# GLA input, gate and output projections as three products of rounded operands instead of full-precision products, with each weight panel's remainder written over the panel in the load ring

## The chip, the cores and the metric

One core of a Trainium2 chip runs the whole program. TensorE multiplies (PE in the rows, PEld for its weight loads), VectorE (DVE) and ScalarE (ACT) do the elementwise work, GpSimd (POOL) does little, and SyncE (SP) issues the loads from HBM. The metric is the device time of one execution in microseconds (us).

## What is computed

Two transformer blocks follow each other on 256 tokens of width 1024, all in float32. The change touches the first layer of the second block, a gated linear attention (GLA). Cut to that:

```
def gla_mixer(h, w_in, w_g2, b_g2, norm_g, w_out):
    proj = h @ w_in
    q, k, v, og, gl = jnp.split(proj, [H * dk, 2 * H * dk, 2 * H * dk + H * dv, 2 * H * dk + 2 * H * dv], axis=-1)
    log_a = jax.nn.log_sigmoid((gl @ w_g2 + b_g2).astype(jnp.float32)) / GLA_GATE_TAU
    ...
    b = jnp.cumsum(log_a.reshape(shp), axis=2)
    q_t = q * jnp.exp(b)
    k_t = k * jnp.exp(-b)
    k_dec = k * jnp.exp(b_last - b)
    scores = jnp.einsum('bnchd,bnmhd->bnhcm', q_t, k_t)
    ...
    o = rmsnorm_2(o, norm_g) * jax.nn.silu(og.reshape(bsz, s_len, H, dv).astype(jnp.float32))
    return (o.reshape(bsz, s_len, H * dv) @ w_out).astype(h.dtype)
```

Here H = 4 heads, dk = 128, dv = 256, and the recurrence runs over chunks of 64 tokens. The layer stands between the feed-forward part of the first block and a retrieval layer over 16384 small experts (`peer`), which takes most of the kernel's time and is not touched.

## The kernel before

Every engine has its own program, written out by hand in order, and they meet through named semaphores. Nothing is reordered by a scheduler: an engine that waits holds back everything behind it.

Weights come as panels of 128 x 2048 float32 (1 MB) into a ring of four slots. SP loads panel n into slot n mod 4 as soon as panel n-4 is freed, and takes the panels in one fixed order. In the GLA layer this order is a panel of `gla_qk` and a panel of `kv_mod` four times, then `gla_v` and `kv_mod` four times, then four of `gla_og`, four of `gla_out` and those of `peer_wq`. A GLA panel is freed when PE has finished its two output tiles (semaphore `proj`). A `kv_mod` panel belongs to another product, which DVE computes one column block at a time (`mod_between` on DVE, L1683 and L1686, eight instructions); it is freed by `mod_acc` when DVE is done, and PE then adds it up over partitions with two small matmuls (L502, `mod_between` on PE) between two GLA panels.

On PE a GLA tile is 8 matmuls of 128 x 128 weights by 256 tokens in float32. The q and k panels go through `proj_cols` (L532), the v panels through `proj_rows` (L542), the og panels through `og_tiles` (L996) spread between the steps of the attention, and the output panels through `proj_cols` again (L532). The tiles alternate between two banks of PSUM, 4 and 5, so that a tile can start only when ACT has copied out (L1139) the tile before the last; for the output panels DVE does this in `residual` (L1728).

Before the panels, the gate projection (`wgl`, 16 columns, L972, then L978) runs. ACT turns its result into the gate's logarithm (L1499 to L1503), DVE sums it up along the tokens (L2305 to L2313) and clears a buffer (L2314), and ACT takes the exponentials (L1508 to L1511, `exps`) between the copies of the q tiles and those of the k tiles. After the attention DVE takes the root of the norm (`roots`, L1775 and L1778) and multiplies the eight blocks of the output by gate and root (`gate_block` L1798, L1809, semaphore `o_done`), which the output projection reads.

Elsewhere the kernel already computes products as three: an operand is rounded to the `f32r` format by a copy on ACT, the remainder is the operand less that copy, taken on DVE or POOL, and PE adds up high x high, high x remainder and remainder x high.

## Time and profile before

| | us |
|---|---|
| median of 3 runs | 2584.69 (2582.22 to 2589.7) |
| the profiled execution's own time | 2585.32 |
| its span in the trace | 2583.5 |
| PE busy | 2500.4 |
| DVE busy | 1780.5 |
| ACT busy | 1239.6 |
| GLA panels in the trace | from 584.9 to 723.9 |

Times in the trace are counted from the span's start. A matmul in float32 shows as two records, so that a tile of 8 is a row with x16; a tile in three products would be x24, one record each. Busy time of PE counts overlapping records once.

### The profile page before, as it was taken

The page shows a single profiled execution, that of the slowest core. Times are in us where ns is not written, and L with a number is a line of the kernel's source. Part 1 is how long each engine was busy: PE and PEld are TensorE (multiplying, and loading weights), DVE is VectorE, ACT ScalarE, POOL GpSimd, SP SyncE. Part 2 cuts the span into 40 slices and gives each one's busy share as a digit, 9 for nine tenths or more (in the row PEclk, how much of TensorE's full clock was granted, in tenths as well). Part 3 has the DMA queues.
Part 4 walks back from the last instruction along what each step waited for, and adds up shares of the span by engine and source line. Part 5 has one row for each costly group of instructions (what it writes and reads, how often), then busy time and mean ns, then how long its engine had stood idle before and what let it go on. Part 6 is the DMA issues. An engine that isn't in the chain of part 4 may idle for free.

```text
span 2583.5 us, 43038 instructions
## 1 busy us (share of the span) xinstructions
PE 2500.4 (97%) x15948; PEld 2246.5 (87%) x15948; DVE 1780.5 (69%) x3565; ACT 1239.6 (48%) x2429; POOL 79.4 (3%) x42
## 2 busy tenths in 40 slices
PE   7999999999999999999999998989999999999997
PEld 4587889988889999999888887789999999888886
DVE  5672668866359977786788875739987787555554
ACT  2322124432234567775444444433557776455444
POOL 0000000000050000000000000022000000000000
PEclk9999999999999999999999999999999999999998
DMA  6562567656343554444777764233554444555553
GB/s 265 197 243 82 204 221 278 237 219 228 115 144 137 181 179 138 141 146 151 259 279 275 274 233 162 82 115 115 180 181 150 144 142 140 193 195 192 190 191 110
DMA packets 65352, 471.70 MB, mean 183 GB/s; under 512 B 7296, under 2 KB 7552, under 8 KB 8240
## 3 DMA queue, kind: packets, MB, share of 16 engines
q1 hardware_dynamic: 64656, 467.85, 50.5%
q8 instruction: 106, 1.74, 0.3%
q10 hardware_dynamic: 272, 1.05, 0.1%
q0 software_dynamic: 272, 0.69, 0.1%
q14 instruction: 46, 0.38, 0.0%
HBM read 468.51 MB, written 1.05 MB: 182 GB/s over the span
## 4 chain that ended last, share of the span: by engine, by line
PE 86%; DVE 6%; DMA 1%; ACT 1%; issue 1%; DVEq 0%; SPq 0%; ACTq 0%
PE bank L745 27%; PE bank L670 27%; PE bank L902 5%; PE bank L682 4%; PE bank L532 4%; PE bank L811 4%; PE bank L697 3%; PE bank L933 2%; PE bank L996 1%; PE bank L542 1%; PE bank L1039 1%; DVE macc L1686 1%; PE bank L516 1%; PE bank L809 1%; PE bank L548 1%
## 5 line engine op out<-in xcount | busy, mean ns | idle before, releaser
L670 PE MATMUL bank<-h_split,t_split 128*128 128x256 f32 x6144 | 772.2, 285 | 6.2 <-DVE t_split L1918 4.9
L670 PEld LDWEIGHTS bank<-h_split,t_split 128*128 128x128 f32 x6144 | 745.5, 191 | 8.5 <-DVE t_split L1918 6.1
L1918 DVE TENSOR_TENSOR t_split<-ring,t_split 128x1024 fp32r<-128x1024 f32 x512 | 624.7, 1221 | 160.7 <-ACT t_split L1212 159.3
L745 PE MATMUL bank<-t_split,w_split 128*128 128x512 f32 x3072 | 703.9, 390 | 0.0
L745 PEld LDWEIGHTS bank<-t_split,w_split 128*128 128x128 f32 x3072 | 574.8, 188 | 118.8
L1217 ACT ACTIVATE t_split<-ring 128x1024 fp32r<-128x1024 f32 x256 | 271.6, 1061 | 357.8 <-PE bank L745 288.7
L1212 ACT ACTIVATE t_split<-ring 128x1024 fp32r<-128x1024 f32 x256 | 271.1, 1059 | 295.8 <-PE bank L670 275.2
L1950 DVE TENSOR_TENSOR w_split<-arena,w_split 128x256 fp32r<-128x256 f32 x256 | 108.8, 425 | 223.5 <-ACT w_split L1219 223.5
L1139 ACT ACTIVATE arena<-bank 128x256 f32<-128x256 f32 (+2 forms) x160 | 64.3, 405 | 326.6 <-PE bank L697 67.0
L1686 DVE SCALAR_TENSOR_TENSOR macc<-ring,cact,macc 128x256 f32<-128x256 f32 x336 | 162.9, 485 | 12.0
L902 PE MATMUL bank<-h_split,wd_split 128*128 128x256 f32 x1056 | 130.1, 284 | 4.0 <-ACT h_split L1439 4.0
L902 PEld LDWEIGHTS bank<-h_split,wd_split 128*128 128x128 f32 x1056 | 127.2, 192 | 5.5 <-issue 4.3
L532 PE MATMUL bank<-arena,ring 128*128 128x256 f32 x512 | 113.7, 381 | 4.2 <-DVE H L2206 2.2
L532 PEld LDWEIGHTS bank<-arena,ring 128*128 128x128 f32 x512 | 96.3, 190 | 18.3 <-DVE H L2206 3.0
L697 PE MATMUL bank<-h_split,q_split 128*128 128x256 f32 x768 | 100.6, 292 | 8.0 <-ACT h_split L1199 7.9
L697 PEld LDWEIGHTS bank<-h_split,q_split 128*128 128x128 f32 x768 | 96.3, 196 | 10.6 <-issue 8.7
L1219 ACT ACTIVATE w_split<-arena 128x256 fp32r (+1 forms) x256 | 102.7, 401 | 0.0
L811 PE MATMUL bank<-H,ring 128*128 128x256 f32 x448 | 100.6, 381 | 1.1 <-DMA ring<-in_w_in 0.8
L811 PEld LDWEIGHTS bank<-H,ring 128*128 128x128 f32 x448 | 83.8, 190 | 12.8 <-DMA ring<-in_w_in 1.0
L532 PE MATMUL bank<-H,ring 128*128 128x512 f32 (+1 forms) x256 | 86.9, 500 | 3.0 <-ACT H L1328 2.3
L2462 POOL TENSOR_TENSOR q_split<-ring,q_split 128x1024 fp32r<-128x1024 f32 x32 | 75.8, 2393 | 317.4 <-ACT q_split L1189 317.4
L1430 ACT ACTIVATE wd_split<-ring 128x1024 fp32r<-128x1024 f32 x44 | 44.1, 1053 | 84.7 <-DMA ring<-in_w_up 55.7
(302 smaller groups left out, 2768.9 us busy)
## 6 DMA issues: line engine op xcount, KB each, us to landing
ring<-in_peer_u SPq DMA_DIRECT2D x128, 1024.0 KB, 4.9
ring<-in_peer_v SPq DMA_DIRECT2D x128, 1024.0 KB, 4.9
ring<-in_w_mod SPq DMA_DIRECT2D x24, 1024.0 KB, 5.1
ring<-in_mod_w SPq DMA_DIRECT2D x24, 1024.0 KB, 4.9
arena<-in_mod_w SPq DMA_DIRECT2D x24, 1024.0 KB, 6.5
ring<-in_w_in SPq DMA_DIRECT2D x22, 1024.0 KB, 4.9
ring<-in_w_up SPq DMA_DIRECT2D x22, 1024.0 KB, 5.1
ring<-in_peer_wq SPq DMA_DIRECT2D x16, 1024.0 KB, 4.9
```

Source lines behind the costliest of these rows:

```text
L532: last = mm(bank[:, 0:width], w[:, k, j * P:(j + 1) * P], rhs(k), start=(k == 0), stop=(k == ks - 1))
L670: last = mm(bank[:, 0:T], u[:, a_, k, :], h_split[:, b_, k, :], start=(k == 0 and a_ + b_ == 0), stop=(k == KT - 1 and a_ == 1))
L682: last = mm(BK[6 + b][:, j * P:(j + 1) * P], P2[b][:, j, :], P1[b][:, j, :], start=True, stop=True)
L697: last = mm(banks[j][:, 0:T], w[:, a_, k, j * P:(j + 1) * P], h_split[:, b_, k, :], start=(first and k == 0), stop=(last_one and k == KT - 1))
L745: last = mm(BK[2 * tt + hf][:, :], w_split[:, j, a_, tt * P:(tt + 1) * P], t_split[:, 1 - j, b_, hf * 512:(hf + 1) * 512], start=(first an ...
L811: last = mm(bank[:, 0:T], w[:, k, half], Hx[:, k, :], start=(k == 0), stop=(k == KT - 1))
L902: last = mm(banks[j][:, 0:T], w[:, a_, k, j * P:(j + 1) * P], h_split[:, b_, k, :], start=(first and k == 0), stop=(last_one and k == KT - 1))
L1212: A(t_split[:, 1 - j, 0, :].rearrange("p (k c) -> p k c", k=KT), ring[:, r, :].rearrange("p (k j c) -> p j k c", k=KT, j=2)[:, j], ACT.Cop ...
L1217: A(t_split[:, 1 - j, 0, :].rearrange("p (k c) -> p k c", k=KT), ring[:, r, :].rearrange("p (j k c) -> p j k c", k=KT, j=2)[:, j], ACT.Cop ...
L1686: ins = STT(acc, w[:, k, :], cact[:, c_col + k:c_col + k + 1], acc, MUL, ADD)
L1918: TT(t_split[:, 1 - j, 1, :].rearrange("p (k c) -> p k c", k=KT), ring[:, r, :].rearrange(view, k=KT, j=2)[:, j], t_split[:, 1 - j, 0, :]. ...
L1950: TT(w_split[:, b % 2, 1, :], arena[:, bass.ds(at * T, T)], w_split[:, b % 2, 0, :].bitcast(f32), SUB).then_inc(sems["w_ready"], 1)
```

## The change

The 16 GLA panels (`GLA[0]` to `GLA[15]`: four q and k, four v, four og, four output) and the gate's weights are multiplied as three products. For panel p, ACT writes the rounded copy in two halves into `g_hi`, which has two buffers (`hi_g`); DVE then writes the remainder over the panel in its ring slot, seen as `ring_lo` (`lo_g`); and PE runs each tile as 24 matmuls (`gla_tile`): it waits for the copy before the first 16 and for the remainder before the last 8 of a panel's first tile. The layer's input gets a remainder too (`h_lo`), and so does the attention's output, block by block (`o_hi` on ACT, `o_lo` on DVE). The program is written in another order only where these calls stand between others. The order of the loads and what frees a slot stay. Lines of before and after differ by some dozens; the main ones after are L1018 (matmuls of a panel), L1173 (copies out of a bank), L1190 (`hi_g`), L1754 and L1757 (`mod_between` on DVE), L1869 (`lo_g`), L1875 (`o_rest`).

```diff
+            pe.wait_ge(sems["wgl_hi"], 1)
             bank = ring_bank()
-            for k in range(KT):
-                fresh(k)
-                last = mm(bank[0:16, 0:T], wgl[:, k, :], hT[:, k, :], start=(k == 0), stop=(k == KT - 1))
+            for a_, b_ in ((0, 0), (1, 0), (0, 1)):
+                if a_ == 1:
+                    pe.wait_ge(sems["wgl_lo"], 1)
+                for k in range(KT):
+                    if a_ == 0:
+                        fresh(k, 1, "h_lo" if b_ else "h")
+                    last = mm(bank[0:16, 0:T], wgl_split[:, a_, k, :], h_split[:, b_, k, :],
+                              start=(a_ == b_ == k == 0), stop=(b_ == 1 and k == KT - 1))
             last.then_inc(sems["turn"], 1)
             pe.wait_ge(sems["wg2_in"], e.more("wg2_in", 16))
             pe.wait_ge(*e.tile_out())
@@ -977,25 +993,42 @@
                 bank = ring_bank()
                 mm(bank[:, 0:T], M3["wg2"][0:16, h * P:(h + 1) * P], M3["glT"][0:16, :], start=True, stop=True).then_inc(sems["turn"], 1)
             mod_start(0)
-            for _ in range(4):
-                proj_cols(1, lambda k: hT[:, k, :], T)
+            def gla_tile(p, j):
+                if j == 0:
+                    pe.wait_ge(sems["gla_hi"], 2 * p + 2)
+                    e.skip(f"loaded{panel[0] % RING}", 16)
+                    panel[0] += 1
+                wh = g_hi[:, p % 2, :].rearrange("p (k c) -> p k c", k=KT)
+                wl = ring_lo[:, GLA[p] % RING, :].rearrange("p (k c) -> p k c", k=KT)
+                part = slice(j * P, (j + 1) * P)
+                bank = ring_bank()
+                for w, b_ in ((wh, 0), (wh, 1), (wl, 0)):
+                    if w is wl and j == 0:
+                        pe.wait_ge(sems["gla_lo"], p + 1)
+                    for k in range(KT):
+                        if p == 12 and j == 0 and w is wh:
+                            fresh(k, 1, "o_lo" if b_ else "o_hi")
+                        if p < 4 or 8 <= p < 12:
+                            lhs, rhs = w[:, k, part], h_split[:, b_, k, :]
+                        elif p < 8:
+                            lhs, rhs = h_split[:, b_, k, part], w[:, k, :]
+                        else:
+                            lhs, rhs = w[:, k, part], (o_lo if b_ else o_hi)[:, k, :]
+                        last = mm(bank[:, 0:T], lhs, rhs, start=(w is wh and b_ == k == 0), stop=(w is wl and k == KT - 1))
+                last.then_inc(sems["proj"], 1)
+            for p in range(8):
+                for j in range(2):
+                    gla_tile(p, j)
                 mod_between(1)
-            for _ in range(4):
-                proj_rows(1, lambda k, tt: hT[:, k, tt * P:(tt + 1) * P], 2)
-                mod_between(1)
-            og_panel = [None, 0]
+            og_now = [0]
             def og_tiles(n):
                 for _ in range(n):
-                    j = og_panel[1] % 2
-                    if j == 0:
-                        og_panel[0] = next_panel().rearrange("p (k c) -> p k c", k=KT)
-                    bank = ring_bank()
-                    for k in range(KT):
-                        last = mm(bank[:, 0:T], og_panel[0][:, k, j * P:(j + 1) * P], hT[:, k, :], start=(k == 0), stop=(k == KT - 1))
-                    last.then_inc(sems["proj"], 1)
-                    og_panel[1] += 1
+                    gla_tile(8 + og_now[0] // 2, og_now[0] % 2)
+                    og_now[0] += 1
             vN3 = M3["vN"].rearrange("p (t n) -> p t n", t=2)
...
+            def hi_g(p):
+                m = GLA[p]
+                act.wait_ge(sems[f"loaded{m % RING}"], 16 * (m // RING + 1))
+                for j in range(2):
+                    half = slice(j * D, (j + 1) * D)
+                    A(g_hi[:, p % 2, half], slot(m)[:, half], ACT.Copy).then_inc(sems["gla_hi"], 1)
             def std_root():
...
@@ -1188,11 +1232,23 @@
                         half = slice(j * D, (j + 1) * D)
                         A(q_split[:, h % 2, 0, half], slot(m)[:, half], ACT.Copy).then_inc(sems["q_hi"], 1)
+                def split_14():
+                    hi_g(14)
+                    hi_q(0)
+                def split_15():
+                    hi_g(15)
+                    hi_q(1)
                 if l == 0:
                     act.wait_ge(sems["o_done"], 1 + 8)
-                hi_q(0)
-                hi_q(1)
-                squares(xT, hP, "proj")
+                    squares(xT, hP, "proj", {1: split_14, 3: split_15})
+                else:
+                    hi_q(0)
+                    hi_q(1)
+                    squares(xT, hP, "proj")
                 std_root()
                 for k in range(KT):
...
@@ -1484,9 +1541,12 @@
             act.wait_ge(sems["var"], e.more("var"))
             A(nrm[:, 1, :], nrm[:, 1, :], ACT.Sqrt, scale=1.0 / D).then_inc(sems["std"], 1)
             A(nrm[:, 0, :], nrm[:, 0, :], ACT.Sqrt).then_inc(sems["xstd"], 1)
+            act.wait_ge(sems["wgl_in"], 16)
+            A(wgl_split[:, 0, :, :], wgl, ACT.Copy).then_inc(sems["wgl_hi"], 1)
             for k in range(KT):
                 act.wait_ge(sems["hs"], e.more("hs"))
-                A(hT[:, k, :], hT[:, k, :], ACT.Identity, bias=modc[:, k:k + 1]).then_inc(sems["h"], 1)
+                A(h_split[:, 0, k, :], hT2[:, k, :], ACT.Identity, bias=modc[:, k:k + 1]).then_inc(sems["h"], 1)
+            hi_g(1)
             evac_gl = 4 + e.tile % 2
             e.tile += 1
             act.wait_ge(sems["turn"], e.more("turn"))
@@ -1503,6 +1563,8 @@
             A(M3["zB"], M3["zB"], ACT.Ln, bias=ones[:, 0:1]).then_inc(sems["zln"], 1)
             for h in range(4):
                 evac("proj", kt(M3["q"], 4)[:, h, :], ACT.Copy, scale=float(P) ** -0.5)
+                if h % 2:
+                    hi_g(2 + h // 2)
             act.wait_ge(sems["expo"], e.more("expo"))
             tau = 1.0 / 16.0
             A(M3["qi0"], M3["cum0"], ACT.Exp, scale=tau)
@@ -1512,16 +1574,21 @@
               scale=tau).then_inc(sems["exps"], 1)
             for h in range(4):
                 evac("proj", kt(M3["k"], 4)[:, h, :], ACT.Copy)
+                if h % 2:
+                    hi_g(4 + h // 2)
             vN3 = M3["vN"].rearrange("p (t n) -> p t n", t=2)
             for c in range(4):
                 for tt in range(2):
                     evac("proj", vN3[:, tt, c * 2 * P:(c + 1) * 2 * P], ACT.Copy)
+                hi_g(6 + c)
             og_now = [0]
             def og_tiles(n):
                 for _ in range(n):
                     evac("proj", kt(M3["og"], 8)[:, og_now[0], :], ACT.Silu)
+                    if og_now[0] % 2 and og_now[0] < 7:
+                        hi_g(10 + og_now[0] // 2)
                     og_now[0] += 1
             lin_turned(M3, 0, 1)
@@ -1535,6 +1602,10 @@
             og_tiles(1)
             lin_root(M3["zA"])
             og_tiles(4)
+            for b in range(KT):
+                act.wait_ge(sems["o_done"], 1 + b + 1)
+                A(o_hi[:, b, :], kt(M3["oT"], 8)[:, b, :], ACT.Copy).then_inc(sems["o_hi"], 1)
+            hi_g(13)
             peer(0, 32, 24)
...
@@ -1787,6 +1860,19 @@
                 ins.then_inc(sems["dve_step"], 1)
                 dve.wait_ge(sems["dve_step"], e.stepped())
                 TT(M1["oT"], M1["oT"], M1["og"], MUL).then_inc(sems["o_done"], 1)
+            def lo_g(p):
+                for j in range(2):
+                    half = slice(j * D, (j + 1) * D)
+                    dve.wait_ge(sems["gla_hi"], 2 * p + j + 1)
+                    ins = TT(ring_lo[:, GLA[p] % RING, half], slot(GLA[p])[:, half], g_hi[:, p % 2, half].bitcast(f32), SUB)
+                ins.then_inc(sems["gla_lo"], 1)
+            def o_rest(b):
+                dve.wait_ge(sems["o_hi"], b + 1)
+                TT(o_lo[:, b, :], kt(M3["oT"], 8)[:, b, :], o_hi[:, b, :].bitcast(f32), SUB).then_inc(sems["o_lo"], 1)
             def gated(root_buf, dv):
@@ -1807,6 +1893,12 @@
                     if b >= 4:
                         dve.wait_ge(sems["dve_step"], gate_block(b))
                     TT(oT[:, b, :], oT[:, b, :], root_buf[:, b // 2 * T:(b // 2 + 1) * T], MUL).then_inc(sems["o_done"], 1)
+                    if b == 1:
+                        lo_g(12)
+                    if b:
+                        o_rest(b - 1)
+                o_rest(7)
+                lo_g(13)
             iota16 = iota[:, 0:16].unsqueeze(1).broadcast_to([P, P, 16])
...
@@ -2291,7 +2383,14 @@
             dve.reciprocal(macc[:, 2, :], nrm[:, 1, :]).then_inc(sems["dve_step"], 1)
             dve.wait_ge(sems["dve_step"], e.stepped())
             for k in range(KT):
-                STT(hT[:, k, :], xT[:, k, :], gain[:, 0, k:k + 1], macc[:, 2, :], MUL, MUL).then_inc(sems["hs"], 1)
+                STT(hT2[:, k, :], xT[:, k, :], gain[:, 0, k:k + 1], macc[:, 2, :], MUL, MUL).then_inc(sems["hs"], 1)
+            dve.wait_ge(sems["wgl_hi"], 1)
+            TT(wgl_split[:, 1, :, :], wgl, wgl_split[:, 0, :, :].bitcast(f32), SUB).then_inc(sems["wgl_lo"], 1)
+            for k in range(KT):
+                dve.wait_ge(sems["h"], GL_H * KT + k + 1)
+                STT(h_split[:, 1, k, :], hT2[:, k, :], modc[:, k:k + 1], h_split[:, 0, k, :].bitcast(f32), ADD, SUB
+                    ).then_inc(sems["h_lo"], 1)
+            lo_g(0)
             dve.wait_ge(sems["xstd"], 1)
             dve.reciprocal(nrm[:, 0, :], nrm[:, 0, :]).then_inc(sems["dve_step"], 1)
             dve.wait_ge(sems["dve_step"], e.stepped())
@@ -2314,6 +2413,7 @@
             dve.memset(M3["sc"], 0.0).then_inc(sems["dve_step"], 1)
             dve.wait_ge(sems["dve_step"], e.stepped())
             for n in range(4):
+                lo_g(n + 1)
                 used(1)
                 mod_between(1, 16)
             e.tiles("proj", 8)
@@ -2323,8 +2423,10 @@
             TT(M3["ki0"], M3["ki0"], M3["k"], MUL)
             TT(M3["kd0"], M3["kd0"], M3["k"], MUL).then_inc(sems["lin_in"], 1)
             for n in range(4):
+                lo_g(n + 5)
                 used(1)
                 mod_between(1, 16)
+            lo_g(9)
             mod_out(0, 16, V("kv_mod_b"), dst=kvm)
             used(4)
             e.tiles("proj", 8)
@@ -2334,8 +2436,15 @@
                 for _ in range(tiles):
                     e.tiles("proj", 1)
                     og_out.append(e.tile_out())
-            lin(M3, 1, 2, M3["zA"], 2 * P, lambda d, h: None, gated)
-            residual("proj", 16)
+            def behind_gated(h):
+                if h == 0:
+                    lo_g(10)
+                if h == 3:
+                    lo_g(11)
+            lin(M3, 1, 2, M3["zA"], 2 * P, lambda d, h: None, gated, behind_gated)
+            residual("proj", 16, also={1: lambda: lo_g(14), 3: lambda: lo_g(15)})
             used(4)
             peer(0)
```

DVE between the end of the gate's sums and the first `kv_mod` panels, before (L2305 to L2313 are the sums, L2314 clears the buffer, L1683 and L1686 are one `kv_mod` panel):

```order
L2305 SCALAR_TENSOR_TENSOR arena<-arena 128x1024
L2309 SCALAR_TENSOR_TENSOR arena<-con,arena 128x256 x4
L2313 TENSOR_TENSOR arena<-arena 128x1024
L2314 MEMSET arena 128x1024
L1683 TENSOR_SCALAR macc<-ring,cact 128x256
L1686 SCALAR_TENSOR_TENSOR macc<-ring,cact,macc 128x256 x7
```

and after:

```order
L2404 SCALAR_TENSOR_TENSOR arena<-arena 128x1024
L2408 SCALAR_TENSOR_TENSOR arena<-con,arena 128x256 x4
L2412 TENSOR_TENSOR arena<-arena 128x1024
L2413 MEMSET arena 128x1024
L1869 TENSOR_TENSOR ring_lo<-ring,g_hi 128x1024 x2
L1754 TENSOR_SCALAR macc<-ring,cact 128x256
L1757 SCALAR_TENSOR_TENSOR macc<-ring,cact,macc 128x256 x7
```

The remainder of panel 1 stands behind the sums and the clearing, and in front of the first `kv_mod` panel; those of panels 2 to 8 stand likewise in front of the later ones.

ACT from the gate's logarithm to the copies of the k tiles, before (the copies out of a bank are L1139; L1508 to L1511 are the exponentials):

```order
L1503 ACTIVATE arena<-arena,con 128x1024
L1139 ACTIVATE arena<-bank 128x256 x4
L1508 ACT_TABLE_LOAD
L1508 ACTIVATE arena<-arena 128x1024
L1509 ACTIVATE arena<-arena 128x1024
L1510 ACTIVATE arena<-arena 128x1024
L1511 ACTIVATE arena<-arena 128x16
L1139 ACTIVATE arena<-bank 128x256 x13
```

and after:

```order
L1563 ACTIVATE arena<-arena,con 128x1024
L1173 ACTIVATE arena<-bank 128x256 x2
L1190 ACTIVATE g_hi<-ring 128x1024 x2
L1173 ACTIVATE arena<-bank 128x256 x2
L1190 ACTIVATE g_hi<-ring 128x1024 x2
L1570 ACT_TABLE_LOAD
L1570 ACTIVATE arena<-arena 128x1024
L1571 ACTIVATE arena<-arena 128x1024
L1572 ACTIVATE arena<-arena 128x1024
L1573 ACTIVATE arena<-arena 128x16
L1173 ACTIVATE arena<-bank 128x256 x2
```

The rounded copies of panels 2 and 3 now stand among the copies of the q tiles, and that of panel 3 in front of the exponentials and of the copies of the k tiles.

DVE behind the root's reciprocal, at the output's blocks, before (L1809 is a block times the root, L1798 a block times its gate):

```order
L1778 RECIPROCAL arena<-arena 128x1024
L1809 TENSOR_TENSOR arena<-arena 128x256 x4
L1798 SCALAR_TENSOR_TENSOR arena<-arena,vec 128x256
L1809 TENSOR_TENSOR arena<-arena 128x256
L1798 SCALAR_TENSOR_TENSOR arena<-arena,vec 128x256
```

and after:

```order
L1851 RECIPROCAL arena<-arena 128x1024
L1895 TENSOR_TENSOR arena<-arena 128x256 x2
L1869 TENSOR_TENSOR ring_lo<-ring,g_hi 128x1024 x2
L1875 TENSOR_TENSOR o_lo<-arena,o_hi 128x256
L1895 TENSOR_TENSOR arena<-arena 128x256
L1875 TENSOR_TENSOR o_lo<-arena,o_hi 128x256
L1895 TENSOR_TENSOR arena<-arena 128x256
L1875 TENSOR_TENSOR o_lo<-arena,o_hi 128x256
L1884 SCALAR_TENSOR_TENSOR arena<-arena,vec 128x256
L1895 TENSOR_TENSOR arena<-arena 128x256
```

Panel 12's remainder and one remainder for each block now stand between the products that finish the blocks.

## Rows read from the trace of the kernel before

**Rows 1.** The page, part 1: busy us, share of the span, instructions.

```profile
PE 2500.4 (97%) x15948; PEld 2246.5 (87%) x15948; DVE 1780.5 (69%) x3565; ACT 1239.6 (48%) x2429; POOL 79.4 (3%) x42
```

**Rows 2.** Windows: us, busy by engine, granted clock, DMA share, GB/s.

```profile
584.00:724.00 140.00, 135.77 (x709) 118.11 (x709) 64.86 (x122) 37.02 (x63) 9.33 (x4) 1.00 0.47 173
```

**Rows 3.** Timeline, two v panels 14.70 us apart: start, length, engine, line, count.

```profile
617.14 7.15 PE L542 MATMUL bank<-ring,H 128*128 128x256 f32 x32
...
631.84 7.15 PE L542 MATMUL bank<-ring,H 128*128 128x256 f32 x32
```

**Rows 4.** Timeline of PE: two tiles in three products, then the keys.

```profile
765.93 5.85 PE L697 MATMUL bank<-h_split,q_split 128*128 128x256 f32 x48
771.62 1.05 PE L651 MATMUL bank<-small,arena 128*128 128x128 f32 x8
```

**Rows 5.** Timeline: a panel of `w_up` split, copy on ACT, remainder on DVE.

```profile
399.94 2.00 ACT L1430 ACTIVATE wd_split<-ring 128x1024 fp32r<-128x1024 f32 x2
...
401.02 2.36 DVE L2220 TENSOR_TENSOR wd_split<-ring,wd_split 128x1024 fp32r<-128x1024 f32 x2
```

**Rows 6.** Timeline: the layer's input, the gate projection, the first GLA panels.

```profile
575.67 3.26 DVE L2294 SCALAR_TENSOR_TENSOR H<-xT,gain,macc 128x256 f32<-128x256 f32 x8
...
576.85 4.92 PE L972 MATMUL bank<-H,arena 128*16 128x256 f32 x16 [4.43 <-ACT H L1489]
...
581.80 0.38 ACT L1493 ACTIVATE arena<-bank 16x256 f32<-16x256 f32 x1 [2.31 <-PE bank L972]
...
584.85 14.05 PE L532 MATMUL bank<-H,ring 128*128 128x256 f32 x64 [0.23 <-ACT arena L1139]
```

**Rows 7.** Timeline: gate's sums, the first `kv_mod` panel, the exponentials.

```profile
591.17 1.22 DVE L2305 SCALAR_TENSOR_TENSOR arena<-arena 128x1024 f32<-128x1024 f32 x1 [7.28 <-ACT arena L1503]
...
597.23 0.35 DVE L1683 TENSOR_SCALAR macc<-ring,cact 128x256 f32<-128x256 f32 x1
...
599.34 1.28 ACT L1508 ACT_TABLE_LOAD   x1
...
601.28 0.61 PE L502 MATMUL bank<-con,macc 128*128 128x1 f32 x4 [2.38 <-DVE macc L1686]
...
603.50 0.21 ACT L1511 ACTIVATE arena<-arena 128x16 f32<-128x16 f32 x1
```

**Rows 8.** Timeline: the load of q/k panel 3, and PE's wait for it.

```profile
601.63 0.43 SPq L354 DMA_DIRECT2D ring<-in_gla_qk  x1
...
609.76 7.17 PE L532 MATMUL bank<-H,ring 128*128 128x256 f32 x32 [0.52 <-DMA ring<-in_gla_qk]
```

**Rows 9.** Issues of 616 to 618: size, us to landing.

```profile
ring<-in_gla_v SPq DMA_DIRECT2D x1, 1024.0 KB, 4.9
ring<-in_kv_mod SPq DMA_DIRECT2D x1, 1024.0 KB, 7.0
```

**Rows 10.** Timeline: the end of the `kv_mod` sums, which PE waits for.

```profile
651.37 0.17 DVE L1695 TENSOR_TENSOR kvm<-bank,vec 128x16 f32<-128x16 f32 x1 [7.93 <-PE bank L502]
```

**Rows 11.** Timeline: og tiles, reciprocal, output blocks, output panels.

```profile
682.24 13.98 PE L996 MATMUL bank<-H,ring 128*128 128x256 f32 x64
...
684.85 6.55 DVE L1778 RECIPROCAL arena<-arena 128x1024 f32<-128x1024 f32 x1 [1.12 <-ACT arena L1180]
...
693.64 0.48 DVE L1798 SCALAR_TENSOR_TENSOR arena<-arena,vec 128x256 f32<-128x256 f32 x1
...
694.50 0.48 DVE L1798 SCALAR_TENSOR_TENSOR arena<-arena,vec 128x256 f32<-128x256 f32 x1
...
696.05 27.79 PE L532 MATMUL bank<-arena,ring 128*128 128x256 f32 x128
...
699.71 0.48 DVE L1728 SCALAR_TENSOR_TENSOR xT<-bank,modc,xT 128x256 f32<-128x256 f32 x1 [2.09 <-PE bank L532]
```

**Rows 12.** Windows behind the norm of `peer`; the last figures: clock, DMA share, GB/s.

```profile
727.00:730.00 3.00, 0.30 (x2) 0.00 (x0) 2.11 (x2) 0.42 (x1) 0.00 (x0) 0.95 1.01 418
730.00:733.00 3.00, 1.73 (x5) 1.36 (x5) 2.96 (x9) 2.38 (x6) 0.00 (x0) 0.50 0.98 415
```

27 lines of the change are left out of this document (21 added, 6 removed).

## Prediction

> **What bounds the kernel now.** I read the page first: PE is busy for 97% of the span, so the time is PE's work plus what PE waits for [rows 1]. The window over the GLA panels gives the same picture for the stretch that changes: in 140 us PE is busy 135.8, DVE 64.9 and ACT 37.0, at the full clock [rows 2]. Then I read the timeline there, engine by engine, because the new work goes to ACT and DVE and what counts is whether it fits where it was put. Two v panels start 14.70 us apart, 7.35 for one, and the kernel spends nearly all of it in matmuls [rows 3]. The reader is to see two places where PE nearly waited already. The first `kv_mod` panel ends on DVE at 601.2, PE had been idle for 2.38 us by then, and the next load in line is issued only then; the load of panel 3 behind it lands 8.1 us after its issue and stops PE at 609.76 [rows 7, 8]. And the output panels start at 696.05, when the blocks they read have only just begun to be ready [rows 11].
>
> **What is saved on PE.** A tile in float32 takes 27.79/8 = 3.47 us with its end, 14.70/2 less the `kv_mod` matmuls of 0.45 gives 6.90 for a panel, 3.45 a tile [rows 3, 11]. Two tiles in three products take 771.62 - 765.93 = 5.69 us, 2.84 a tile [rows 4]. So 32 tiles save 32 x 0.61 = 19.5 us, if nothing waits. The granted clock was full at both places.
>
> The Trainium skill, in "FP8 and Floating Point Precision", section "TensorE Precision Notes", says that a true float32 product goes through the array in four passes. Three single passes would by that rule cost 3/4 of 6.90, 5.18 a panel, and the sum for 16 panels would be 27.6 us instead of 19.5. The rows say less, since a pass of the rounded operands takes 5.69/48 = 0.119 us and a quarter of a float32 product 0.108.
>
> **What is added.** Each panel costs ACT 2.0 us (copy) and DVE 2.4 us (remainder, the second half ending 2.36 after the first began) [rows 5]: 32 and 38 us over the layer. I follow the dates of the trace forward, and write "late" for the shift against before.
>
> 1. Gate. The input's remainders come on DVE behind the eight products that end at 578.9: 8 x 0.41 = 3.3 us plus the gate weights' remainder, so to 582.4, where the gate matmuls now end at 581.8 [rows 6]. They are cheap themselves; ACT's copy starts about 1 us late, and so does all behind it. The first panel starts at 585.8.
>
> 2. Gate's sums. DVE starts them at 591.2 + 0.9 and is 6.0 us in them and the clearing (591.17 to 597.23) [rows 7], then takes the remainder of panel 1: 592.1 + 6.0 + 2.4 = 600.5. PE has finished panel 0 at 591.5, waits 1 us for a bank (ACT is in the logarithm until 592), runs the first 16 matmuls of panel 1 until 594.3, and then waits 6.2 us. The panel ends at 600.5 + 0.9 + 2.8 = 604.3. Queued behind the remainder is `kv_mod` panel 0: 4.0 us [rows 7], done at 604.6, before at 601.2. PE goes on at 605.0 where it was 601.75: 3.2 late.
>
> 3. The load of panel 3 stands behind a load that waits for that `kv_mod` panel, so it is 3.4 late too and lands at 609.7 + 3.4 = 613.1 [rows 8]. Now PE doesn't read it directly. ACT waits for it in program order, copies it until 615.1, and only then takes the exponentials, 603.7 - 599.3 = 4.4 us [rows 7], to 619.5, and only behind them copies the k tile out of the bank that panel 3 needs. PE has been done with panel 2 since 611.0. It starts panel 3 at 620.0, before 609.8: 10.2 late, 9 us of waiting.
>
> 4. v panels. The round of one slot is: panel done, load 4.9 to 7.0 us [rows 9], copy 2.0, bank freed 0.5, panel 5.7, and it serves two panels: 6.5 to 7.6 us a panel. DVE needs 2.4 + 4.0 = 6.4. I take 7.0 against 7.35, so five panels give back 3 us of which DVE takes 1.5 to 3 again, because the last `kv_mod` sum and the remainder of panel 9 stand ahead of L1695, on which PE waits already [rows 10]. Late: 9 to 10 at 651.4.
>
> 5. og tiles. Seven of the eight run before the root is done and save 4.3 us; about 1.8 goes to waits for copies of panels 9 and 11. In front of the root DVE also waits for panel 11's copy and takes its remainder, 1.9 us. So PE ends the og tiles at about 703 (before 696.0, 7 late), the reciprocal ends at 702 (before 691.4, 10.5 late).
>
> 6. First output tile. Before, a late block costs DVE 694.50 - 693.64 = 0.86 us, and the first tile ends 8.3 after the reciprocal [rows 11]. After: two blocks 0.7, remainder of panel 12 2.4, two blocks and three remainders 1.9, four blocks at 0.86 + 0.37 with remainders 5.0, last remainder 0.5, sum 10.5; then PE's part, 1.9. The tile ends 12.4 after the reciprocal, at 714.3; before 699.5: 14.8 late. PE is mostly idle from 703 to 712.
>
> 7. The seven output tiles behind it save 4.3 and lose 0.6 to a bank that DVE frees late behind remainder 14. Late: 11.
>
> 8. Clock. After 4.43 us of idle PE at 572 to 577, and after the idle stretch from 727.3, the granted clock was 0.50, the lower of its two levels (1.2 GHz), while the 2.38 us of idle at 599 left it at 1.00 [rows 6, 7, 12]. Steps 2, 3 and 6 each make 6 to 9 us of idle. At half clock 3 us of work cost 3 more; one such stretch in each of the three places, part of it hidden behind DVE, costs 2 to 6 us. I take 3.5. The lower end is nothing, since no row shows what follows an interrupted wait.
>
> Sum: -19.5 on PE, about +30 of new waits and their followers, +3.5 clock: 14.5 us later at the end of the layer. The rest of the kernel starts from there unchanged: `peer`'s first panels are copied while the last output tiles run. The profiled execution took 2585.3, the median is 2584.7; I forecast 2599.2, which I round to 2599.
>
> **Rivals.** A difference under 0.3% (7.8 us) can't be told from no change here.
>
> A. The work hides. By shares DVE would be at 64.9 + 38 and ACT at 37 + 32 of about 125 us, so both have room [rows 2], and PE would keep its 19.5 less step 1 and a third of step 6: 2584.7 - 19.5 + 5 = 2570. It needs remainder 1 on DVE before 594.3 and copy 3 on ACT without waiting for its load. Against it stand the order rows: the remainder is behind the sums, the copy before the exponentials. The point from which it decides: if steps 2, 3 and 6 cost under 11 us together instead of 26, the kernel is faster.
>
> B. The waits of steps 2 and 3 are there, but the loads land sooner (4.9 us each once the pair is apart) and the v panels run at 6.5, with no clock loss: 14.5 - 3.5 - 2.5 - 2.5 = 6 late, 2591: no change that could be told.
>
> C. The clock falls longer (two stretches at each place, as 730 to 733 stayed low under light work [rows 12]) and the loads keep at 7.0: 14.5 + 3 + 3.5 = 21 late, 2606.
>
> D. A pass of rounded operands costs only a quarter of a float32 product, so a tile takes 2.6 us: 0.25 less in the 14 og and output tiles that PE itself sets, the others wait anyway, 3.5 us, 2595.7. The same shape took 2.84 in [rows 4], so it gets 0.02. This is what the four passes of the Trainium skill's page named above would give.
>
> **How the numbers follow.** Forecast 0.60 (2592 to 2604), B 0.17, C 0.12, A 0.09, D 0.02. The likeliest case's own range is 2592 to 2604. The range for 8 in 10 leaves out A and the edge of C: 2587 to 2606. Faster by more than 0.3%: 0.08, from A. Within: 0.20, from B, the low end of the forecast and the weak end of A. Slower: 0.72.
>
> **What the profile would show.** Step 2: PE waits about 6 us for DVE's `ring_lo` near 594 to 600. Step 3: PE waits at panel 3, released by ACT, with the exponentials just before it. Step 4: v panels about 7 us apart, with waits on `g_hi`. Step 6: PE waits on `o_hi` and `o_lo` for 7 to 10 us near 703 to 712. Step 8: granted clock 0.5 in windows behind these. If PE's waits in the layer sum to under 15 us, or a tile takes other than 2.84 us at the full clock, I am wrong.

## The result and the profile after

The changed kernel takes 2609.53 us (median of 4 runs, 2606.05 to 2610.6), the kernel before 2584.97 on the same chip (4 runs, 2582.22 to 2589.7): ratio 1.0094, 95% interval 1.0081 to 1.0108. It is 24.6 us slower, where 14.5 had been forecast, and lies above the range (2587 to 2606). Of all executions reported in this document one, of the kernel of e3, lies far from the rest, at 9749.39 us; it is left out of every comparison.

The page of the changed kernel, part 1, against [rows 1]:

```profile
PE 2503.6 (96%) x16212; PEld 2259.9 (87%) x16212; DVE 1826.9 (70%) x3614; ACT 1273.2 (49%) x2470; POOL 80.6 (3%) x42
```

PE has 264 records more (8 for each of 32 tiles, 8 for the gate projection), DVE 46 us and ACT 34 us more. That PE is busy 3 us *longer*, where 19.5 us of work was to go, is the first thing to explain. The layer is compared from the gate projection's first matmul to `peer`'s first query product, in the windows of that stretch, before and after (us, busy by engine, clock, DMA share, GB/s):

```profile
576.85:731.27 154.42, 145.57 (x744) 123.50 (x745) 75.73 (x143) 43.71 (x78) 9.33 (x4) 0.99 0.47 173
```

```profile
577.08:757.02 179.94, 146.83 (x1008) 134.94 (x1009) 122.25 (x192) 75.51 (x116) 10.58 (x4) 0.85 0.41 148
```

The stretch grows by 25.5 us, and from there to the end both kernels take nearly the same in these two profiles (1852.2 and 1851.8). PE's idle time in it goes from 154.42 - 145.57 = 8.9 to 33.1 us, 24.3 more. Its busy time should have fallen by 19.5 and rose by 1.3: what was to be saved is lost again while the granted clock is 0.85 on average against 0.99, 20.8 us of busy time.

PE's timeline at the waits of steps 2, 3, 4, 6 and 7, against [rows 7, 8, 10, 11]:

```profile
602.94 2.08 PE L1018 MATMUL bank<-h_split,ring_lo 128*128 128x256 f32 x8 [5.58 <-DVE ring_lo L1869]
604.82 3.62 PE L1018 MATMUL bank<-h_split,g_hi 128*128 128x256 f32 x16
...
609.80 2.13 PE L1018 MATMUL bank<-h_split,g_hi 128*128 128x256 f32 x16
...
621.34 3.75 PE L1018 MATMUL bank<-h_split,g_hi 128*128 128x256 f32 x16 [5.30 <-ACT arena L1173]
...
652.88 3.52 PE L1018 MATMUL bank<-g_hi,h_split 128*128 128x256 f32 x16 [3.85 <-ACT arena L1173]
...
666.41 1.72 PE L588 MATMUL bank<-arena 64*128 64x256 f32 x6 [1.70 <-DVE kvm L1766]
...
711.11 0.60 PE L1018 MATMUL bank<-o_hi,g_hi 128*128 128x256 f32 x2 [0.87 <-ACT o_hi L1607]
713.34 0.38 PE L1018 MATMUL bank<-o_hi,g_hi 128*128 128x256 f32 x1 [1.63 <-ACT o_hi L1607]
...
722.57 1.91 PE L1018 MATMUL bank<-o_hi,g_hi 128*128 128x256 f32 x8
...
742.34 2.04 PE L1018 MATMUL bank<-o_hi,g_hi 128*128 128x256 f32 x8 [4.38 <-DVE xT L1799]
```

The same 16 matmuls take 2.13 us at 609.80 and 3.62 or 3.75 behind each of the first waits. Windows of the same trace (the third figure from the end is the clock) show why:

```profile
592.00:602.00 10.00, 5.37 (x46) 5.17 (x44) 7.27 (x9) 4.46 (x6) 0.00 (x0) 1.00 0.31 107
602.00:609.00 7.00, 6.06 (x29) 6.06 (x30) 6.75 (x12) 0.92 (x2) 0.00 (x0) 0.52 0.14 39
609.00:619.00 10.00, 7.04 (x62) 6.95 (x60) 7.02 (x14) 4.82 (x6) 0.00 (x0) 1.00 0.96 358
619.00:626.00 7.00, 4.66 (x22) 4.70 (x23) 6.21 (x11) 4.36 (x7) 0.00 (x0) 0.51 0.55 193
```

The clock is at its lower level (1.2 GHz) when PE comes back at 602.94 and at 621.34 from waits of 5.58 and 5.30 us, and at the upper one (2.4 GHz) in the windows before these. Added over the stretch it is at half for 52.7 us, before for 4.2.

ACT in front of step 3's wait, and DVE and POOL in front of step 7's, in their timelines:

```profile
614.54 2.00 ACT L1190 ACTIVATE g_hi<-ring 128x1024 fp32r<-128x1024 f32 x2 [4.52 <-DMA ring<-in_gla_qk]
616.56 1.28 ACT L1570 ACT_TABLE_LOAD   x1
...
620.83 0.63 ACT L1173 ACTIVATE arena<-bank 128x256 f32<-128x256 f32 x2
```

```profile
728.54 2.36 DVE L1869 TENSOR_TENSOR ring_lo<-ring,g_hi 128x1024 fp32r<-128x1024 f32 x2 [1.43 <-ACT g_hi L1190]
...
735.12 6.69 DVE L1869 TENSOR_TENSOR ring_lo<-ring,g_hi 128x1024 fp32r<-128x1024 f32 x2 [2.32 <-ACT g_hi L1190]
```

```profile
732.66 4.78 POOL L2571 TENSOR_TENSOR q_split<-ring,q_split 128x1024 fp32r<-128x1024 f32 x2 [164.22 <-ACT q_split L1233]
...
738.24 5.80 POOL L2571 TENSOR_TENSOR q_split<-ring,q_split 128x1024 fp32r<-128x1024 f32 x2 [0.79 <-ACT q_split L1233]
```

What the rows of DVE and POOL show was not foreseen: the remainder of panel 15 takes DVE 6.69 us, that of panel 14 took 2.36, and what differs is POOL, which is taking the remainders of `peer`'s first two query panels. PE, two tiles on, waits 4.38 us for the bank that DVE frees late.

### The profile page after: what moved, and what is told of

Read it like the earlier page. It is cut to its first block, busy times and chain, and to the rows that moved or that the text cites. A ratio compares the mean times of both kernels' runs of the same rounds, so it can differ in the third digit from the quotient of the medians.

```text
span 2608.8 us, 43658 instructions
## 1 busy us (share of the span) xinstructions
PE 2503.6 (96%) x16212; PEld 2259.9 (87%) x16212; DVE 1826.9 (70%) x3614; ACT 1273.2 (49%) x2470; POOL 80.6 (3%) x42
## 3 DMA queue, kind: packets, MB, share of 16 engines
q10 hardware_dynamic: 272, 1.05, 0.1%
HBM read 468.51 MB, written 1.05 MB: 180 GB/s over the span
## 4 chain that ended last, share of the span: by engine, by line
PE 87%; DVE 8%; DMA 2%; ACT 2%; issue 1%; SPq 0%; DVEq 0%; ACTq 0%
PE bank L755 27%; PE bank L680 27%; PE bank L912 5%; PE bank L692 4%; PE bank L542 4%; PE bank L821 4%; PE bank L707 3%; PE bank L943 2%; PE bank L1018 2%; DVE macc L1757 1%; PE bank L526 1%; PE bank L552 1%; PE bank L1073 1%; DVE ring_lo L1869 1%; PE bank L819 1%
## 5 line engine op out<-in xcount | busy, mean ns | idle before, releaser
L1173 ACT ACTIVATE arena<-bank 128x256 f32<-128x256 f32 (+2 forms) x160 | 63.7, 404 | 288.9 <-PE bank L707 67.0
L1757 DVE SCALAR_TENSOR_TENSOR macc<-ring,cact,macc 128x256 f32<-128x256 f32 x336 | 162.9, 485 | 12.0
L542 PE MATMUL bank<-arena,ring 128*128 128x256 f32 x384 | 85.9, 382 | 4.2 <-DVE H L2298 2.2
L542 PEld LDWEIGHTS bank<-arena,ring 128*128 128x128 f32 x384 | 72.0, 190 | 15.0 <-DVE H L2298 3.0
L2098 DVE SCALAR_TENSOR_TENSOR macc<-arena,cact,macc 128x256 f32<-128x256 f32 x168 | 81.0, 482 | 3.4
```

Of the source, the lines that this page charges most:

```text
L542: last = mm(bank[:, 0:width], w[:, k, j * P:(j + 1) * P], rhs(k), start=(k == 0), stop=(k == ks - 1))
L1757: ins = STT(acc, w[:, k, :], cact[:, c_col + k:c_col + k + 1], acc, MUL, ADD)
```

## The experiments

Each ran in 3 rounds beside the kernel before (its medians there 2584.11 to 2585.93) unless it says otherwise. The table cuts the stretch at the state products (PE L588) and at the end of the reciprocal. us, and in brackets those of them at half clock:

| kernel | gate to states | to reciprocal's end | to `peer` | whole | median | ratio to before |
|---|---|---|---|---|---|---|
| before | 74.75 (2.7) | 39.80 (0) | 39.87 (1.6) | 154.4 | 2584.97 | |
| before, again | 76.14 (11.8) | 39.80 (0) | 39.87 (0.7) | 155.8 | | |
| changed | 89.33 (30.7) | 42.69 (6.8) | 47.92 (15.1) | 179.9 | 2609.53 | 1.0094 |
| changed, again | 86.95 (28.9) | 42.57 (6.5) | 49.07 (17.1) | 178.6 | | |
| e1 | 84.83 (23.4) | 42.70 (6.8) | 49.19 (17.1) | 176.7 | 2603.10 | 1.0073 [1.0056, 1.0090] |
| e2 | 84.13 (23.4) | 42.68 (6.8) | 44.55 (11.4) | 171.4 | 2600.89 | 1.0064 [1.0047, 1.0081] |
| e3 | 87.02 (29.0) | 42.56 (6.5) | 41.71 (10.2) | 171.3 | 2600.74 | 1.0065 [1.0045, 1.0085] |
| e4 | 87.54 (15.9) | 42.25 (5.8) | 48.73 (17.1) | 178.5 | 2606.08 | 1.0086 [1.0069, 1.0103] |
| e5 | 85.33 (36.0) | 39.06 (3.4) | 44.61 (17.1) | 169.0 | 2597.91 | 1.0051 [1.0034, 1.0068] |
| e6 | 86.69 (25.5) | 42.72 (6.8) | 37.25 (1.2) | 166.7 | 2592.58 | 1.0037 [1.0022, 1.0053] |
| e7 | 84.05 (27.3) | 39.61 (3.4) | 41.06 (7.0) | 164.7 | 2589.50 | 1.0015 [1.0005, 1.0024] |
| e8 | 85.02 (6.8) | 39.68 (0) | 47.53 (7.6) | 172.2 | 2599.70 | 1.0057 [1.0040, 1.0074] |
| e9 | 80.16 (15.0) | 38.09 (0) | 34.82 (1.5) | 153.1 | 2582.83 | 0.9996 [0.9987, 1.0005] |
| e10 | 84.03 (27.3) | 39.64 (3.4) | 37.25 (0) | 160.9 | 2587.60 | 1.0010 [1.0001, 1.0020] |
| e11 | 87.76 (26.8) | 41.12 (6.8) | 48.27 (13.8) | 177.2 | 2605.68 | 1.0081 [1.0066, 1.0097] |
| e12 | 76.60 (11.8) | 38.09 (0) | 34.82 (1.2) | 149.5 | 2578.27 | 0.9977 [0.9968, 0.9986] |

One profile of a kernel against another of the same differs by 1 to 2.5 us in the first part, so a difference under 2 us there is not read. Each profile is of a single execution, and what lies behind the stretch counts too. In the twelve profiles of kernels that split the q, k and v panels it took 1847.4 to 1852.4 us, in the four others 1852.2 to 1852.9, though the code there is the same; why stays open. So the medians of most variants lie closer to the kernel before than their stretches say, and both are given where it matters. A number of us from the medians is the difference of two ratios times 2585.

**e1: remainder of panel 1 ahead of gate's sums (step 2).**

```diff
             lo_g(0)
+            lo_g(1)
             dve.wait_ge(sems["xstd"], 1)
...
-                lo_g(n + 1)
+                if n:
+                    lo_g(n + 1)
```

> The remainder of panel 1 is taken right behind that of panel 0, ahead of the gate's sums. Theory (queues in order, one late item makes the next late): PE's 5.6 us wait for ring_lo near 597 to 603 goes, but kv_mod panel 0 ends only 2.3 us sooner, so the load of panel 3 and everything behind it come 2 to 3 us sooner; the wait at panel 3 grows by about what was saved. Total 2 to 3 us under the changed kernel. Rival (each wait costs its own length, with the half clock behind it): 7 to 8 us less.

3.2 us less in the profile, 1.9 against the second profile of the change, 5.4 by the medians; 2 to 3 were expected. PE's wait for `ring_lo` is gone, but it waits 3.37 us for the first `kv_mod` sum instead: the wait of before [rows 7], and 1 us more. The wait at panel 3 grew only from 5.30 to 5.81, not by what was saved. What step 2 had put on the remainder was right; the wait under it stays.

**e2: copy of panel 3 behind the exponentials and the first k copy (step 3).**

```diff
-                if h % 2:
-                    hi_g(2 + h // 2)
+                if h == 1:
+                    hi_g(2)
...
                 evac("proj", kt(M3["k"], 4)[:, h, :], ACT.Copy)
+                if h == 0:
+                    hi_g(3)
```

> On ACT the rounded copy of panel 3 stands behind the exponentials and the first k tile instead of ahead of them. Theory: the exponentials run from about 610 to 614.4 while the load is under way, the copy ends at 616.5, and PE starts panel 3 at about 616.6 instead of 621.3; total 4 to 6 us less, with part of the half clock behind it. Rival (the load's landing or DVE's remainder 3 sets the pace of the layer anyway): under 1.5 us less at the end of the layer.

PE starts panel 3 at 613.67 and waits 0.58 where it had waited 5.30:

```profile
608.38 1.06 ACT L1570 ACTIVATE arena<-arena 128x1024 f32<-128x1024 f32 x1
...
611.62 1.99 ACT L1190 ACTIVATE g_hi<-ring 128x1024 fp32r<-128x1024 f32 x2
```

ACT takes the exponentials while the load is still on its way. The panels behind give much of it back (waits of 2.46 and 3.52 at L1173): at the states 2.8 to 5.2 us are left, where 4 to 6 were expected for the whole. The other 3.4 to 4.5 of its 8.5 us (7.8 by the medians) come from the last part and were not foreseen. They hang on a near tie in the collision that e3 is about. DVE starts the remainder 2.46 us behind POOL in both kernels, and the first half takes 3.4 us in both. In the change POOL's next half starts at 738.24, ahead of DVE's second half at 738.45, and that half takes 3.36 us. In e2 both start at the same time, and it is POOL that takes longer:

```profile
730.32 1.21 DVE L1871 TENSOR_TENSOR ring_lo<-ring,g_hi 128x1024 fp32r<-128x1024 f32 x1
```

```profile
730.32 3.44 POOL L2573 TENSOR_TENSOR q_split<-ring,q_split 128x1024 fp32r<-128x1024 f32 x1 [1.01 <-ACT q_split L1233]
```

So the pair on DVE takes 4.55 us instead of 6.69. In the other profiles with this order of the copies (e1, e4, e5, e8, e11 and the second of the change) both halves are slow: this part of e2's gain is luck of the order, 0.2 us wide.

**e3: copies for `peer`'s query panels behind panel 15's copy (step 7).**

```diff
                     hi_g(14)
-                    hi_q(0)
...
                     hi_g(15)
+                    hi_q(0)
                     hi_q(1)
```

> The copy of query panel 0, behind which GpSimd takes its remainder, stands behind the copy of GLA panel 15 instead of that of panel 14. Theory (DVE's subtraction of panel 15 took 6.7 us instead of 2.4 because GpSimd's subtraction ran at the same time): the two no longer meet, remainder 15 takes 2.4 us, PE's 4.4 us wait behind it goes, 4 to 5 us less in all. Rival (DVE was slowed by something else there, such as the loads or ACT): remainder 15 stays above 5 us and the total stays.

The last part is 6.2 to 7.4 us shorter, more than the 4 to 5 expected, since the half clock behind the wait goes with it (from 741.9 to 745.3 in the change, none there in e3). By the medians it is 7.5. POOL now starts at 731.48, when DVE is nearly done:

```profile
729.53 2.36 DVE L1869 TENSOR_TENSOR ring_lo<-ring,g_hi 128x1024 fp32r<-128x1024 f32 x2 [1.43 <-ACT g_hi L1190]
...
733.31 0.48 DVE L1799 SCALAR_TENSOR_TENSOR xT<-bank,modc,xT 128x256 f32<-128x256 f32 x1 [1.02 <-PE bank L1018]
```

So the same two instructions take 2.36 us when POOL starts behind them (e3), 4.55 when POOL is ahead of the first alone (e2), and 6.69 when it is ahead of each (the change). ACT and the loads have the same work in all three. The wait of 4.38 and the half clock behind it are this collision.

**e4 and e8: idle matmuls while PE waits (step 8).** They write into a bank that nothing reads then. e4 has them at steps 2 and 3, e8, in smaller portions, also ahead of the gate, the last v panel, the states and between the blocks of the first output tile.

```diff
+                if j == 0 and p == 3:
+                    warm(44)
...
+                        if p == 1:
+                            warm(44)
                         pe.wait_ge(sems["gla_lo"], p + 1)
```

> Two times 44 matmuls whose result nobody reads (into a free bank) fill PE's waits at panel 1 and at panel 3; nothing else changes. It tells the price of the half clock behind a wait. Theory (clock is a surcharge of some us, the queues are the main cost): the granted clock stays 1.00 behind both, panel 1 ends 3 us sooner but the next load does not, panel 3 ends 2 us sooner, 1 to 3 us less in all. Rival (the half clock is what the forecast missed, 7 to 10 us): 5 us or more less.

> Matmuls of constants into a bank that is free fill PE's waits ahead of the gate, at panels 1, 3 and 7, ahead of the first states and between the output's blocks; the order is that of the changed kernel. It prices the half clock of the whole layer, 51 us of it against 3 in the kernel before. Theory: a good part was hidden behind DVE, so 5 to 8 us less. Rival (it was all exposed): 15 us or more less; other rival (filler delays what it fills): no gain or slower.

In e4 no half clock is left from 592 to 649, and the stretch is 1.4 us shorter (2.1 by the medians); the wait at the second v panel grew from 0.90 to 2.65, and one of 1.05 for a `kv_mod` sum came. In e8 it is at half for 14.4 us instead of 52.7 and the stretch is 7.7 us shorter, though the wait behind panel 15 grew from 4.38 to 6.09 us, as PE is there sooner. Against the second profile of the change it is 6.4 us, by the medians 9.6. So 38 of the 52.7 us at half clock cost 6 to 10 us, about 8. PE's busy time in the change is far more over its due, 20.8 us. The waits that grew in e8 speak for the rest being slowed work in front of a wait that ends when another engine does.

**e5: most of the product with the remainder left out.** Of the product with `ring_lo`, only the first and the last of 8 blocks are taken in each tile, and the rest of that product is left out; all waits are kept.

```diff
-                    for k in range(KT):
+                    for k in range(KT) if w is wh else (0, KT - 1):
```

> Every GLA tile takes only 2 of its 8 matmuls of the weights' remainder, so 18 matmuls instead of 24; that part of the product is left out. The copies, remainders, loads and waits stay. TensorE's work falls by 32 x 6 x 0.118 = 22.7 us. Theory (outside the og and output tiles PE is not what sets the pace): the 15 tiles that PE paces give back about 0.7 each and the 16 of q, k and v nearly nothing, 10 to 14 us less in all. Rival (PE's work is the bound, the price of the passes was mis-sized): 20 us or more less.

22.7 us of PE work less (6 of 24 matmuls a tile, 32 tiles, 0.118 us each) make the stretch 10.9 us shorter (11.1 by the medians), as expected. Waits for copies and remainders grow to fill the rest (8.56 us at panel 3, 6.46 behind panel 15). About half of PE's time counts in this schedule.

**e6: output projection in full precision (steps 6 and 7).** As before the change; gate, q, k, v and og panels stay in three products.

```diff
-            for p in range(12, 16):
-                for j in range(2):
-                    gla_tile(p, j)
+            proj_cols(4, lambda k: o8[:, k, :], T, first=True, name="o_done")
```

> Only the gate, q, k, v and og panels are multiplied as three products; the four output panels stay in full precision, without copies and remainders. Theory: the chain from the reciprocal to the first output tile falls from 13.7 to about 8.3 us, seven tiles cost 0.6 each more (4.3), the collision of DVE and GpSimd and its 4.4 us wait go, and so does the half clock behind both: 6 to 10 us less than the changed kernel. The q, k, v stretch stays late by about 15 us. Rival (the output panels are where the change gains): 2 to 5 us more.

13.3 us shorter (14.7 by the medians), where only 6 to 10 had been expected: 37.25 us from the reciprocal to `peer` instead of 47.9 to 49.1. So splitting the output projection, a fourth of the tiles, costs 10.7 to 11.8 us here. The part up to the states stays 12 us late.

**e11: remainder of panel 11 behind the gate products (step 5).**

```diff
                     gate_block(b)
+                lo_g(11)
                 roots(root_buf, dv)
...
-                if h == 3:
-                    lo_g(11)
```

> The change with the remainder of panel 11 moved behind the eight gate products of the output, nothing else. My sum gave its place ahead of them 1.9 us (a wait of VectorE for ScalarE's copy). In the trace of the change that remainder's row has 7.38 us of idle time before it, ended by the copy. Theory 1 (the wait is on the path to the reciprocal and all of what it holds there is given back): 2 to 6 us less, the stretch 174 to 178. Rival (VectorE would wait for the score products or the root anyway): under 1 us.

The part from the states to the reciprocal is 1.5 us shorter; my sum had 1.9 for this. The stretch is 2.8 us shorter, but only 1.4 against the second profile of the change, 3.4 by the medians: the low end of the 2 to 6 expected, or under it.

**e7: e1, e2, e3 and e11 together.**

> Four moves together: remainder 1 ahead of the gate's sums, copy 3 behind the exponentials, query panel 0's copy behind panel 15's, and remainder 11 behind the four gate products. Theory: the sum of the single ones with one or two us lost where two meet, 13 to 18 us under the changed kernel, so still 7 to 12 above the kernel before, because the v panels' ring and the root's chain stay. Rival (the order was all of it): at or under the kernel before, 24 us less.

15.2 us shorter, 13 to 18 were expected. The single gains add up to some 23, but e2 and e3 both count part of the collision, and the waits behind a moved one take up some of it, as in e2. In the stretch 10 us against before are left, 9 of them ahead of the states. By the medians only 3.9 us are left (interval 1.3 to 6.2), less than the 7 to 12 expected; the part behind the stretch, 1848.6 us in e7's profile and 1852.2 before, makes up for some of it.

Of the 9 us ahead of the states one wait can be followed further, at the last v panel (3.67 us). Its load is issued at 636.26, once DVE has ended the fifth `kv_mod` panel at 635.86 (before: 624.79) and that slot's load has gone out; it lands 8.4 us later, and ACT copies it before it frees the bank:

```profile
644.64 2.00 ACT L1190 ACTIVATE g_hi<-ring 128x1024 fp32r<-128x1024 f32 x2 [7.39 <-DMA ring<-in_gla_v]
```

No run moves this chain, so what it costs is not shown.

**e10: e6 with the moves of e1, e2 and e11.**

> The output projection in full precision (as in the run that did that alone), with the remainder of panel 1 ahead of the gate's sums, the copy of panel 3 behind the exponentials and the remainder of panel 11 behind the gate products. Theory 1 (each piece is a delay of the path and they add up, less what one hides of the next): the stretch was 166.7 with the output in full precision; 3.2 and part of the 8.5 come off, as much as all four moves took together less the query's (15.2 less some 6.5 is 8 to 9): 157 to 160, the time 2584 to 2588. Rival (the moves only help where the output is split, since its start is what waits): the stretch stays at 164 to 167 and the time at 2590 to 2593.

160.9 and 2587.6: the delays add up nearly as the theory had it (157 to 160, 2584 to 2588). What is left in the stretch is the 9 us ahead of the states, less 2.6 in the last part, where, it seems, the og tiles' saving is now collected.

**e9 and e12: only where there is cover.** Split are the og panels 8 to 11 and output panels 13 to 15. Gate, q, k, v and panel 12 are in full precision. The input's rounded copy and remainder are made during the v panels, the remainder over `hT` once its last reader is done; e12 also takes the remainder of panel 8 ahead of it.

```diff
-            for p in range(8):
-                for j in range(2):
-                    gla_tile(p, j)
+            for _ in range(4):
+                proj_cols(1, lambda k: hT[:, k, :], T)
...
+            for _ in range(4):
+                proj_rows(1, lambda k, tt: hT[:, k, tt * P:(tt + 1) * P], 2)
...
+            lo_g(8)
             e.tiles("proj", 8)
             dve.wait_ge(*e.tile_out())
+            for j in range(2):
...
+                TT(h_split[:, 0, s, :], hT[:, s, :], h_split[:, 1, s, :].bitcast(f32), SUB).then_inc(sems["wgl_lo"], 1)
```

> Only the og panels 8 to 11 and the output panels 13 to 15 are products of rounded operands; the gate projection, the panels of q, k and v and output panel 12 are in full precision as before. The rounded copy of the input and its remainder are made while TensorE works on the v panels, those of the output projection's input beside panel 12, and the remainder of panel 11 stands behind the gate products, the query copies behind panel 15's. Theory 1 (the loss lies where new copies and remainders stand on the path that sets the end; where they have work to lie beside, a split tile's 0.61 us are a gain): 8 og tiles and 6 output tiles less 0.61 each is 8.5, less some 3 for a wait for the first output remainder and for half clock behind it; the layer's stretch ends 148 to 152 (154.4 before, 179.9 in the change), the time 2578 to 2584. Rival (the loss is in the form itself: what rounded operands cost in clock or in the weight loads of the tiles): these seven panels lose in proportion, 7/16 of the 25 or some 8 to 11 us, the time 2593 to 2597.

> As the run that splits only the og panels and the output panels 13 to 15, with the remainder of panel 8 ahead of the input's remainder on VectorE (there PE waited 3.01 us for it). In that run the sum without the clock was 154.4 less 8.5 plus 1.1 of waits, 147; the stretch took 153.1, with 12.3 us more at half clock than in the profile of before (6.1 us of work), 6.8 of it at 582.8 to 589.6, where the code is that of before. Theory 1 (that half clock at the opening is of the execution, not of the code): PE waits 2 or less at panel 8, the stretch 147 to 152, the time 2579 to 2583. Rival (any wait saved comes back, as the clock falls anyway): the stretch stays at 153, the time at 2583.

Both ran in 5 rounds. e9's profile has the stretch 1.3 us under that of before, where 148 to 152 had been expected, and its time can't be told from that of before (0.9987 to 1.0005). The rival, a loss of 8 to 11 us by the form itself, is excluded. PE waited 3.01 us for panel 8's remainder at its first og tile. In e12 it waits 0.30 there:

```profile
645.24 2.36 DVE L1876 TENSOR_TENSOR ring_lo<-ring,g_hi 128x1024 fp32r<-128x1024 f32 x2 [1.60 <-ACT g_hi L1199]
647.51 2.35 DVE L2430 TENSOR_TENSOR h_split<-H,h_split 128x1024 fp32r<-128x1024 f32 x2
```

```profile
648.51 1.11 PE L1020 MATMUL bank<-h_split,ring_lo 128*128 128x256 f32 x8
649.92 1.21 PE L1020 MATMUL bank<-h_split,g_hi 128*128 128x256 f32 x8 [0.30 <-DVE h_split L2430]
```

The stretch is 149.5 us (147 to 152 expected) and the time 2578.27, just under the 2579 to 2583 expected and 0.23% under before (interval 0.14% to 0.32%). It is the best of the versions here, and faster than both kernels, if only by 6 us. The last two parts give 1.7 + 5.05 = 6.8 of the 14 x 0.61 = 8.5 us that the tiles save.

**e13 and e14: both kernels profiled once more**, one look each.

> The kernel before, profiled once more. In its first profile the clock was at half from 576.1 to 579.5 at the layer's opening and nowhere else up to the first query product; in every other run whose opening is untouched or nearly so it was at half for 10.2 to 13.6 us there. If that is of the execution: here 10 us or more at half clock at the opening, and the stretch 157 to 159 instead of 154.4. If it is of the code: 3.4 us again and 154 to 155.

> The change, profiled once more. Its first profile has 50.9 us at half clock in the layer's stretch of 179.9. If most of it hangs on the code's waits, it stays: 40 to 55 us in the same places (behind the waits for panel 1's remainder, panel 3's start, the last v panel, the states, the first output tile, panel 15), and the stretch 177 to 181. If it is of the execution: under 35 us, and the stretch under 174.

In e13 the opening is at half clock for 11.8 us instead of 2.7, so that part is of the execution, not of the code. (e9 and e12, whose opening is that of before, have 11.6 and 11.8, so the first profile of before is the exception.) It cost only 1.4 us, since PE's 2.38 us of waiting for the first `kv_mod` sum [rows 7] vanished in it; 157 to 159 was expected, 155.8 came. In e14 the half clock behind the waits stays, 52.5 us in the same places (the table's 52.7 in the first profile): that is of the code.

## Why the forecast had the sign and missed the size

With both second profiles the loss is 10.8 + 2.8 + 9.2 = 22.8 us by parts, with the first ones 14.6 + 2.9 + 8.05 = 25.5. The forecast's parts, without its 3.5 for the clock, were 9.5, 1 and 0.5. In both pairs it is the last part that missed most, by 7.5 to 8.7 us.

- **Saved on PE.** Right in size: a tile takes 595.34 - 592.51 = 2.83 us at the full clock. e12 collects 6.8 of its 8.5 us.
- **Step 1.** In the first profile 2 us more than forecast: the first panel starts at 587.85, the clock being at half from 578.1 to 591.7. Between the second profiles it is 585.65 against 584.44, 1.2 us late, as forecast.
- **Step 2.** Mechanism right (a wait of 5.58 for `ring_lo`, 6.2 forecast; e1). PE goes on at 602.94, forecast 600.5 (600.74 in e14). The panel behind starts 8.0 late instead of 3.2: 2.4 us are carried over from step 1, and the rest of panel 1, 2.8 us longer than forecast, runs at half clock: that part is step 8's.
- **Step 3.** Right in the chain on ACT (e2), and PE starts panel 3 at 621.34, forecast 620.0; but the load came on time by luck. It was issued at 609.63, 4.6 us later than forecast, as PE freed panel 1 late at half clock, and took 4.9 us where 8.1 had been taken, so it landed at 614.52, forecast 613.1. PE came late too and waited 5.30 us, not 9.
- **Step 4.** The round held (panels 6 to 10 us apart, the slow ones behind waits of 0.90 and 3.85), but nothing was made up: PE passes the states 14.8 late, 12.3 between the second profiles, where 9 to 10 were forecast. The sum had a slip of its own: five panels at 7.0 against 7.35 give back 1.75 us, not 3.
- **Step 5.** Reciprocal 17.7 late, forecast 10.5; 5 of the 7 us between them are carried over from the states. The remainder's own 1.9 was 1.5 (e11). What was missing is half clock from 666.8 to 673.6: in e8, without it, this part took 39.68 us, 3 less.
- **Step 6.** The first output tile ends 722.8 - 709.1 = 13.7 after the reciprocal, forecast 12.4, on the blocks' order as worked out; its last two products are at half clock (1.91 instead of 1.11).
- **Step 7 failed.** "The seven output tiles behind it save 4.3 and lose 0.6": they took 34.2 us with the norm, before 731.27 - 699.5 = 31.8, so 2.4 more instead of 3.7 less. The wait of 4.38 is DVE held back by POOL (e3), the rest half clock. In e3, without both, they took 746.39 - 718.35 = 28.0, the 3.7 less of the forecast. The working took DVE's remainder at the 2.36 of [rows 5] wherever it stood, and never asked what POOL did beside it; that the change puts the copy of the first query panel, and POOL's work behind it, ahead of panel 15's copy stood in the diff (`split_14`, `split_15`).
- **Step 8 failed in size.** "I take 3.5": about 8 by e8 (6 to 10), with part of the half clock left. The sum let the clock fall in up to three places; the trace shows six beside the opening, one behind each of the waits of 5.58, 5.30, 3.85 and 4.38 us, one behind the blocks of the first output tile and one behind a wait of only 1.70.

Of the rivals, C came nearest (2606): its mechanism, the clock, is shown; its slow loads were not tested (those of the v panels took 4.7 to 7.9 us in the change), and it had nothing of the collision, so that its nearness is in part luck. A is excluded for the change as written, and e12 shows its point: with cover, the same form gains. B's quick v panels didn't come, and D's price is not that of a tile (2.83).

The loss is thus explained by parts as follows, in the profiles: output projection 11 to 12 us (e6), of which the collision with its half clock 6 to 7 (e3); copy of panel 3 about 3 to 5 (e2); remainder of panel 1 2 to 3 (e1); remainder of panel 11 1.5 (e11). These overlap and don't sum to the loss. With all moved (e7), some 9 us stay ahead of the states. What sets those was not taken apart and stays open: waits of 3.55 for the `kv_mod` sum and 3.67 at the last v panel are left, and 27 us at half clock, of which 14 at the opening.
